# Attention inside a hybrid decoder layer: values as matmul weights in two column halves, four blocks at a time, then turned back

## The chip, the cores and the metric

The kernel runs on one core of a Trainium2 chip. The core has a matmul engine (TensorE, "PE" in the profile; its weight loads are listed apart as "PEld"), a vector engine (DVE), a scalar engine (ACT), GpSimd (POOL) and a queue engine (SP) that here only issues DMAs. Each engine runs its own instructions in order and they meet at semaphores. The metric is the device time of one whole execution in microseconds; lower is better.

## The reference

One layer at sequence length 2048 and width 1024, all in fp32: RMSNorm, one projection, eight retention heads beside eight heads of dilated sliding-window attention, output projection, then a SwiGLU block. The change touches only the attention:

```python
# per pattern (window, dilation) in (128,1), (512,4), (2048,16); blocks of 128 queries
s = einsum('brhnqd,brhnkd->brhnqk', qb, kcat) * (D ** -0.5)   # own block of keys and the one before
s = where(mask, s, -inf); m = max(s); p = exp(s - m); den = sum(p)
o = einsum('brhnqk,brhnkd->brhnqd', p, vcat) / den
lse = m + log(den)
# then: w = softmax(stack(lses)); out = sum(w * stack(outs))
```

## The kernel before

Three stages follow each other on the core: the projection (`project`, to about 555 us), the attention (`attention`, to about 849 us), and the rest (`mix`: retention, combination, output projection; `ffn`).

`attention` works on pairs of heads. There are NU = 4 pairs ("units") and, for each, NB = 48 blocks of 128 queries: 16 of dilation 1, 16 of dilation 4, 16 of dilation 16; so ALL = 192 blocks, numbered n. A block with a block of keys before it has two key blocks of 128 ("full": 27 of the 48, namely 15 of the first 16 and 12 of the next 16), the others have one ("half": 21, and all of the last 16). Per block n:

- `scores(n)` on PE (L763): for two heads, two matmuls each with the queries as weights and the keys as the moving operand (fp32r), into one of NS = 3 PSUM banks.
- DVE (L822): scales, adds the mask, takes the minimum of the negated scores, writes `prob[n % 4]` and the minimum into `orow[n % RING]`; waits for `turned` of block n-4 because `prob` has four buffers.
- ACT (L851): exp over `prob`, two instructions.
- `turn(n)` on PE (L775): 2 or 4 transposes of `prob` into one of TURNED = 3 banks. It waits for exp of block n and for the copy of block n-3.
- `copy_turned(n)`: PSUM to `probT`; even blocks on DVE (L813), odd blocks on ACT (L841). On DVE it stands right behind the maxima of block n+2, so DVE waits there for the turn.
- `values(n)` on PE (L787): `probT` as weights (128 columns), the values with a column of ones beside each head as moving operand (65 columns, fp32): 2 or 4 matmuls, each shown as two passes. The ones give the denominator.
- `copy_out(n)` on ACT (L845): result and denominator (130 columns) into `orow`; SP stores the row block to `att_out` (L714).

The order on PE is written out by hand: in step n, `scores(n+4)`, `turn(n+1)`, `values(n-1)`. On DVE: maxima of n, then (n even) `copy_turned(n-2)`; in the last unit also `early_vector`, which for even j from 24 to 40 (not 32) rounds an eighth of the next stage's weights (L1127). On ACT: exp of n, then (n odd) `copy_turned(n-2)`, then `copy_out(n-4)`. POOL reorders queries and keys for the dilated patterns beside all this (L881 to L885).

`mix` uses the matmul array in tiles in two places: L1253 with `tile_position=(h*32, 0)` (32 rows by 128 columns, 128 moving columns) and L1229 with `tile_position=(0, h*32)` (128 rows by 32 columns, 64 moving columns), both fp32.

Of the kernel before, what the change touches and what calls it, by code (L numbers as in the profile page):

```python
# [9 lines left out]
ACT = mybir.ActivationFunctionType  # L10
# [4 lines left out]
P = 128  # L15
# [7 lines left out]
ATT_HEADS, ATT_D = 8, 64  # L23
# [623 lines left out]
def attention(nc, D, bank, first, mixed):  # L647
# [6 lines left out]
    NU = ATT_HEADS // 2  # L654
    ALL = NU * NB
    SCALE = ATT_D ** -0.5
    NS, AHEAD, TURNED = 3, 4, 3
    RING = 16
    OW = ATT_D + 1
    NEAR = CHUNKS  # L660
    m = Mem(nc, None, "at")
    ident, mask, vblk = (first[n] for n in ("ident", "mask", "vblk"))
# [1 line left out]
    def place(name, shape, frame, offset=0, dt=F32):  # L664
        return nc.alloc_sbuf_tensor_at(f"at_{name}", shape, dt, offset=FRAMES + frame * FRAME + offset)
# [2 lines left out]
    k_by4 = place("k_by4", [P, 2, 2, SEQ], 8, dt=F32R)  # L668
    q_by16 = place("q_by16", [P, 2, SEQ], 12, dt=F32R)
    prob = place("prob", [P, 4, 2, 2 * P], 14)  # L670
    probT = place("probT", [P, TURNED, 2, 2, P], 15)
    orow = place("orow", [P, RING, AO_W], 15, 6144)
    s_ps = bank[:, 0:NS, :].rearrange("p n (h k) -> p n h k", h=2)
    t_ps = bank[:, NS:NS + TURNED, :].rearrange("p n (h b q) -> p n h b q", h=2, b=2)
    o_ps = bank[:, NS + TURNED:8, :].rearrange("p n (h k) -> p n h k", h=2)
    consts, qk_first, qk_rest, v_loaded = (first[n] for n in ("consts", "qk_first", "qk_rest", "v_loaded"))
    permuted = m.sem("permuted")
    scored, maxed, exped = m.sem("scored"), m.sem("maxed"), m.sem("exped")
    turned = m.sem("turned")
    turn_copied = m.sems("turn_copied", 2)  # L680
    valued, o_copied = m.sem("valued"), m.sem("o_copied")
    waited = m.sem("waited")
    stored = m.sems("stored", RING)

    C_O = 2
    C_SCORED, C_PERMUTED = 1, 1
    BY_4, BY_16 = 6, 8
    keys = [slice(0, 2 * P) if b[3] else slice(P, 2 * P) for b in blocks]
# [20 lines left out]
    def sync(sp):  # L709
        def store(u, j):  # L710
            p, t0, d, _ = blocks[j]
            sp.wait_ge(o_copied, NB * u + j + 1 + C_O)
            dst = D["att_out"][p, t0:t0 + d * (P - 1) + 1:d, :]
            sp.dma_start(dst[:, bass.ds(u * AO_W, AO_W)], orow[:, j % RING, :]).then_inc(stored[j % RING], 16)  # L714

        def unit(u, s, more=True):

            sp.wait_ge(permuted, BY_16 * u + C_PERMUTED)
            sp.sem_inc(waited, 1)
            sp.wait_ge(scored, NB * u + C_SCORED)  # L720
            sp.sem_inc(waited, 1)
            for j in range(NB):
                store(u, j)
                if more:
                    for n in range(2 * QK_DMAS):
                        if (n // 2 if n < QK_DMAS else QK_DMAS // 2 + 5 * (n - QK_DMAS) // 2) == j:
                            load_qk(sp, D, first, u + 1, 1 - s, n)
                if more and j and j % 4 == 0:
                    load_values(sp, D, first, u + 1, j // 4 - 1)
                if not more:  # L730
                    mixed["early_sync"](sp, j, permuted, BY_16 * NU + C_PERMUTED)
            if more:
                load_values(sp, D, first, u + 1, VALUE_LOADS - 1)

        for r, free in enumerate(first["row_free"]):
            sp.wait_ge(free, first["rows_stored"])
        with sp.Fori(0, NU // 2 - 1) as it:
            unit(2 * it, 0)
            unit(2 * it + 1, 1)
        unit(NU - 2, 0)  # L740
        unit(NU - 1, 1, more=False)

    def copied(eng, n):
        eng.wait_ge(turn_copied[n % 2], n // 2 + 1)

    def tensor(pe):
        pe.sem_inc(scored, C_SCORED)

        def scores(n):
            u, j = divmod(n, NB)  # L750
            if j == 0:
                pe.wait_ge(qk_first, 16 * QK_DMAS * u + 16 * QK_DMAS)
            if j == GROUP // P:
                pe.wait_ge(qk_rest, 16 * QK_DMAS * u + 16 * QK_DMAS)
            if j == NEAR:
                pe.wait_ge(permuted, BY_16 * u + BY_4 + C_PERMUTED)
            if j == 2 * NEAR:
                pe.wait_ge(permuted, BY_16 * u + BY_16 + C_PERMUTED)
            if n >= NS:
                pe.wait_ge(maxed, n - NS + 1)  # L760
            for h in range(2):
                for lower in range(2):
                    last = nc.tensor.matmul(s_ps[:, n % NS, h, keys[j]], query(u % 2, j, h), key(u % 2, j, h, lower),  # L763
                                            start=lower == 0, stop=lower == 1)
            last.then_inc(scored, 1)

        def turn(n):
            j = n % NB
            pe.wait_ge(exped, n + 1)
            if n >= TURNED:  # L770
                copied(pe, n - TURNED)
            for h in range(2):
                for kb in range(2):
                    if kb == 1 or blocks[j][3]:
                        last = nc.tensor.transpose(t_ps[:, n % TURNED, h, kb, :], prob[:, n % 4, h, kb * P:(kb + 1) * P], ident[:])  # L775
            last.then_inc(turned, 1)

        def values(n):
            u, j = divmod(n, NB)
            if j % 4 == 0:  # L780
                pe.wait_ge(v_loaded[j // 4], 16 * u + 16)
            copied(pe, n)
            pe.wait_ge(o_copied, n + 1)
            first = 0 if blocks[j][3] else 1
            for h in range(2):
                for kb in range(first, 2):
                    last = nc.tensor.matmul(o_ps[:, n % 2, h, 0:OW], probT[:, n % TURNED, h, kb, :], vblk[:, j - 1 + kb, h, :],  # L787
                                            start=kb == first, stop=kb == 1)
            last.then_inc(valued, 1)

        for n in range(AHEAD):
            scores(n)
        turn(0)
        for n in range(ALL):
            if n + AHEAD < ALL:
                scores(n + AHEAD)
            if n + 1 < ALL:
                turn(n + 1)
            if n:
                values(n - 1)  # L800
        values(ALL - 1)

    def vector(dve):
        for r in range(RING):
            dve.sem_inc(stored[r], 16)
        dve.wait_ge(consts, 16)

        def copy_turned(n):
            if n >= TURNED:
                dve.wait_ge(valued, n - TURNED + 1)  # L810
            dve.wait_ge(turned, n + 1)
            kb = 0 if blocks[n % NB][3] else 1
            nc.vector.tensor_copy(probT[:, n % TURNED, :, kb:, :], t_ps[:, n % TURNED, :, kb:, :]).then_inc(turn_copied[0], 1)  # L813

        for n in range(ALL):
            j = n % NB
            dve.wait_ge(scored, n + 1 + C_SCORED)
            if n >= 4:
                dve.wait_ge(turned, n - 3)
            dve.wait_ge(stored[n % RING], 16 * (n // RING) + 16)  # L820
            for h in range(2):
                last = nc.vector.tensor_tensor_reduce(  # L822
                    out=prob[:, n % 4, h, keys[j]], in0=s_ps[:, n % NS, h, keys[j]], in1=mask[:, keys[j]],
                    scale=-SCALE, scalar=-3 * NEG, op0=ALU.add, op1=ALU.min,
                    accum_out=orow[:, n % RING, 2 * OW + h:2 * OW + h + 1])
            last.then_inc(maxed, 1)
            if n >= 2 and n % 2 == 0:
                copy_turned(n - 2)
            if n >= ALL - NB:
                mixed["early_vector"](dve, j, permuted, BY_16 * NU + C_PERMUTED)  # L830
        copy_turned(ALL - 2)

    def scalar(act):
        act.sem_inc(o_copied, C_O)

        def copy_turned(n):
            if n >= TURNED:
                act.wait_ge(valued, n - TURNED + 1)
            act.wait_ge(turned, n + 1)
            kb = 0 if blocks[n % NB][3] else 1  # L840
            nc.scalar.activation(probT[:, n % TURNED, :, kb:, :], t_ps[:, n % TURNED, :, kb:, :], ACT.Copy).then_inc(turn_copied[1], 1)  # L841

        def copy_out(n):
            act.wait_ge(valued, n + 1)
            nc.scalar.activation(orow[:, n % RING, 0:2 * OW].rearrange("p (h c) -> p h c", h=2), o_ps[:, n % 2, :, 0:OW], ACT.Copy).then_inc(o_copied, 1)  # L845

        for n in range(ALL):
            act.wait_ge(maxed, n + 1)
            for h in range(2):
                pr = prob[:, n % 4, h, keys[n % NB]]  # L850
                last = nc.scalar.activation(pr, pr, ACT.Exp, bias=orow[:, n % RING, 2 * OW + h:2 * OW + h + 1], scale=-1.0)  # L851
            last.then_inc(exped, 1)
            if n >= 2 and n % 2 == 1:
                copy_turned(n - 2)
            if n >= 4:
                copy_out(n - 4)
        copy_turned(ALL - 1)
        for n in range(ALL - 4, ALL):
            copy_out(n)

    def gpsimd(pool):
        pool.sem_inc(permuted, C_PERMUTED)
# [1664 lines left out]
```

## Time and profile before

| | us |
|---|---|
| median of 3 runs | 2446.33 (2446.18 to 2450.53) |
| the profiled execution | 2445.58 |
| its span (first to last instruction) | 2443.8 |
| attention, about | 556 to 849 |

Busy time over the span is 2380.5 us (97%) on PE, 1429.3 (58%) on DVE, 926.1 (38%) on ACT and 596.0 (24%) on POOL. A matmul instruction of fp32 operands appears as two passes, each with a weight load. The duration of a pass includes its way through the array, and passes overlap, so the cost of one is the distance between the starts of two, not its duration. In a timeline, equal neighbours are merged into one row: its start, the time from the first start to the last end, and the count; the last one starts one duration before the row's end.

### The profile page before, as it was taken

How to read it: one execution, taken by the hardware profiler on the slowest of the kernel's cores; microseconds unless marked ns; L12 is line 12 of the kernel's file. 1: busy time of each engine (PE TensorE's matmuls, PEld its weight loads, DVE VectorE, ACT ScalarE, POOL GpSimd, SP SyncE). 2: the span in 40 equal slices, each digit the busy share in tenths (PEclk: the TensorE clock that was granted, in tenths of full speed). 3: DMA queues.
4: the chain of work that ended last, by engine and by line, in shares of the span. 5: the costliest groups of instructions: out<-in, count | busy, mean ns of one | idle time of the engine just before them, and what ended most of it. 6: DMA issues, size and time to landing. Idle time of an engine off the chain costs nothing. (4 is left out here: it accounts for less than half of the span.)

```text
span 2443.8 us, 35931 instructions
## 1 busy us (share of the span) xinstructions
PE 2380.5 (97%) x12432; PEld 2019.1 (83%) x12432; DVE 1429.3 (58%) x2671; ACT 926.1 (38%) x1790; POOL 596.0 (24%) x365
## 2 busy tenths in 40 slices
PE   7999999999999989999899999989999999999998
PEld 6888888889999978887788888878888887888887
DVE  4322346635555568788666656776665665455655
ACT  4401122217777613234433333533333343322332
POOL 0089555525553456662000000000000000000001
PEclk9999999999999979999999999999999999999999
DMA  5423224466776445555333333433333335445655
GB/s 182 128 77 108 69 75 114 120 185 175 182 177 176 136 151 178 191 181 203 125 95 105 103 106 107 129 124 91 106 93 117 107 112 202 142 146 197 235 205 188
DMA packets 308890, 344.92 MB, mean 141 GB/s; under 512 B 17072, under 2 KB 239920, under 8 KB 308528
## 3 DMA queue, kind: packets, MB, share of 16 engines
q1 hardware_dynamic: 308784, 343.54, 45.9%
q8 instruction: 62, 1.02, 0.2%
q14 instruction: 44, 0.36, 0.1%
HBM read 231.41 MB, written 112.07 MB: 141 GB/s over the span
## 5 line engine op out<-in xcount | busy, mean ns | idle before, releaser
L1812 PE MATMUL fin_psum_bank<-ff_b_hi,ff_w_hi 128*128 128x512 f32 x1232 | 482.4, 392 | 18.7 <-issue 8.6
L1812 PE MATMUL fin_psum_bank<-ff_b_hi,ff_w_lo 128*128 128x512 f32 x1232 | 481.4, 391 | 0.0
L1812 PE MATMUL fin_psum_bank<-ff_b_lo,ff_w_hi 128*128 128x512 f32 x1232 | 481.3, 391 | 0.0
L2111 POOL TENSOR_TENSOR ff_ssq<-ff_ssq,ff_minus_half 128x1 f32<-128x1 f32 x16 | 14.8, 926 | 1265.8 <-DVE ff_ssq L2379 1265.8
L1812 PEld LDWEIGHTS fin_psum_bank<-ff_b_hi,ff_w_hi 128*128 128x128 f32 x1232 | 232.7, 189 | 69.3 <-issue 9.0
L1812 PEld LDWEIGHTS fin_psum_bank<-ff_b_lo,ff_w_hi 128*128 128x128 f32 x1232 | 232.7, 189 | 48.5
L1812 PEld LDWEIGHTS fin_psum_bank<-ff_b_hi,ff_w_lo 128*128 128x128 f32 x1232 | 232.4, 189 | 48.7
L1894 PE MATMUL fin_psum_bank<-ff_down_hi,ff_act_hi 128*128 128x512 f32 x616 | 240.4, 390 | 2.2 <-DVE ff_act_lo L2143 2.2
L1894 PE MATMUL fin_psum_bank<-ff_down_hi,ff_act_lo 128*128 128x512 f32 x616 | 240.3, 390 | 0.0
L1894 PE MATMUL fin_psum_bank<-ff_down_lo,ff_act_hi 128*128 128x512 f32 x616 | 240.2, 390 | 0.0
L2115 DVE TENSOR_TENSOR ff_w_lo<-ff_raw,ff_w_hi 128x512 fp32r<-128x512 f32 x176 | 120.9, 688 | 145.6 <-ACT ff_w_hi L1905 145.5
L460 PE MATMUL pr_psum_acc<-pr_hT_hi,pr_w_hi 128*128 128x512 f32 x512 | 199.2, 389 | 0.0
L460 PE MATMUL pr_psum_acc<-pr_hT_lo,pr_w_hi 128*128 128x512 f32 x512 | 199.2, 389 | 0.0
L460 PE MATMUL pr_psum_acc<-pr_hT_hi,pr_w_lo 128*128 128x512 f32 x512 | 199.2, 389 | 0.0
L851 ACT ACTIVATE at_prob<-at_prob,at_orow 128x256 f32<-128x256 f32 (+1 forms) x384 | 155.4, 454 | 36.3 <-DVE at_orow L822 35.1
L1953 ACT ACTIVATE ff_taken<-fin_psum_bank 128x512 f32<-128x512 f32 x132 | 78.9, 597 | 227.1 <-PE fin_psum_bank L1812 222.1
L1925 ACT ACTIVATE ff_act_hi<-ff_act_raw 128x1408 fp32r<-128x1408 f32 x56 | 77.4, 1382 | 216.3 <-DMA ff_act_raw<-a_parts 216.3
L787 PE MATMUL fin_psum_bank<-vblk,at_probT 128*128 128x65 f32 x1200 | 155.4, 267 | 0.3
L1905 ACT ACTIVATE ff_w_hi<-ff_raw 128x512 fp32r<-128x512 f32 x176 | 109.9, 627 | 108.0 <-PE fin_psum_bank L1812 103.0
L787 PEld LDWEIGHTS fin_psum_bank<-vblk,at_probT 128*128 128x128 f32 x1200 | 148.9, 192 | 1.1 <-ACT at_probT L841 0.9
L2115 DVE TENSOR_TENSOR ff_w_lo<-ff_sums,ff_w_hi 128x512 fp32r<-128x512 f32 x132 | 90.6, 689 | 91.5 <-ACT ff_w_hi L1905 91.5
L822 DVE CUSTOM_DVE_ANT_0 at_prob<-fin_psum_bank,mask 128x256 f32<-128x256 f32 (+1 forms) x384 | 119.8, 360 | 36.0 <-PE fin_psum_bank L763 34.5
(206 smaller groups left out, 4557.8 us busy)
## 6 DMA issues: line engine op xcount, KB each, us to landing
ff_act_raw<-a_parts SPq DMA_DIRECT2D x56, 704.0 KB, 4.1
ff_raw<-in_w_gate SPq DMA_DIRECT2D x22, 1024.0 KB, 5.9
ff_raw<-in_w_up SPq DMA_DIRECT2D x22, 1024.0 KB, 5.3
a_parts<-ff_a_sum SPq DMA_DIRECT2D x88, 256.0 KB, 6.1
ff_down_raw<-in_w_down SPq DMA_DIRECT2D x77, 256.0 KB, 4.7
a_parts<-ff_up SPq DMA_DIRECT2D x66, 256.0 KB, 2.3
att_out<-at_orow SPq DMA_DIRECT2D x192, 66.0 KB, 3.0
mx_att_in<-att_out SPq DMA_DIRECT2D x16, 792.0 KB, 4.8
```

Source lines behind the costliest of these rows:

```text
L460: last = nc.tensor.matmul(acc[:, g, :], w[s][:, k, :], h[:, k, t], start=k == 0 and n == 0, stop=k == KT - 1 and n == 2)
L787: last = nc.tensor.matmul(o_ps[:, n % 2, h, 0:OW], probT[:, n % TURNED, h, kb, :], vblk[:, j - 1 + kb, h, :], start=kb == first, stop=kb == 1)
L822: last = nc.vector.tensor_tensor_reduce(out=prob[:, n % 4, h, keys[j]], in0=s_ps[:, n % NS, h, keys[j]], in1=mask[:, keys[j]], scale=-SCAL ...
L851: last = nc.scalar.activation(pr, pr, ACT.Exp, bias=orow[:, n % RING, 2 * OW + h:2 * OW + h + 1], scale=-1.0)
L1812: last = nc.tensor.matmul(to, w[:, i, k, :], b[i][:, k, :], start=fresh and k == 0 and which == 0, stop=k == KH - 1 and which == 2, skip_g ...
L1894: last = nc.tensor.matmul(bank[:, ORDER[n], :], a[t % 3][:, k, :], w[o % 2][k][:], start=k == 0 and which == 0, stop=k == PAIRS - 1 and wh ...
L1905: nc.scalar.activation(w_hi[:, i], weight(i, s), ACT.Copy).then_inc(w_hi_done[i], 1)
L1925: nc.scalar.activation(act_hi[t % 3][:], act_raw[t % 3][:], ACT.Copy).then_inc(act_hi_done, 1)
L1953: nc.scalar.activation(taken[:, i, :], X[s], ACT.Copy).then_inc(snapped, 1)
L2111: nc.gpsimd.tensor_tensor(ssq[:, n % 2, 1:2], ssq[:, n % 2, 1:2], minus_half[:], ALU.pow).then_inc(rooted, 1)
L2115: nc.vector.tensor_tensor(w_lo[:, i], weight(i, s), w_hi[:, i].bitcast(F32), ALU.subtract).then_inc(w_lo_done[i], 1)
```

## The change

`values` now works on quads of four blocks. The values become the weights, 64 columns for each head, head 0 in columns 0 to 63 of the array and head 1 in columns 64 to 127 (`tile_position=(0, h * ATT_D)`), and `probT` is the moving operand (128 columns). The result of a quad is one PSUM bank `oT_ps`, with the head's dimensions on the partitions. DVE copies it to SBUF (`lift`), PE turns it back with four transposes (`turn_back`), and ACT copies four row blocks at once into `orow` (`copy_out`). The denominator is no longer a column of ones: the exp instruction sums its output itself (`accum_out`). `probT` gets KEPT = 6 buffers instead of 3.

```diff
-        def values(n):
-            ...
-            copied(pe, n)
-            pe.wait_ge(o_copied, n + 1)
-            for h in range(2):
-                for kb in range(first, 2):
-                    last = nc.tensor.matmul(o_ps[:, n % 2, h, 0:OW], probT[:, n % TURNED, h, kb, :], vblk[:, j - 1 + kb, h, :],
-                                            start=kb == first, stop=kb == 1)
+        def values(q):
+            if q:
+                pe.wait_ge(lifted, q)
+            ...
+            for i in range(QUAD):
+                n, j = QUAD * q + i, j0 + i
+                copied(pe, n)
+                first = 0 if blocks[j][3] else 1
                 for kb in range(first, 2):
+                    for h in range(2):
+                        rows = slice(h * ATT_D, (h + 1) * ATT_D)
+                        last = nc.tensor.matmul(oT_ps[rows, i * P:(i + 1) * P], vblk[:, j - 1 + kb, h, 1 - h:1 - h + ATT_D],
+                                                probT[:, n % KEPT, h, kb, :], start=kb == first, stop=kb == 1,
+                                                tile_position=(0, h * ATT_D), skip_group_check=True)
+        def turn_back(q):
+            pe.wait_ge(lifted, q + 1)
+            if q:
+                pe.wait_ge(o_copied, q)
+            for i in range(QUAD):
+                last = nc.tensor.transpose(o_ps[:, i, :], oT[:, q % 2, i * P:(i + 1) * P], ident[:])
...
-            if n:
-                values(n - 1)
+            if n % QUAD == 0 and n:
+                values(n // QUAD - 1)
+            if n % QUAD == 2 and n > QUAD + 2 - 1:
+                turn_back(n // QUAD - 1)
...
+        def lift(q):
+            if q >= 2:
+                dve.wait_ge(turned_back, q - 1)
+            dve.wait_ge(valued, q + 1)
+            nc.vector.tensor_copy(oT[:, q % 2, :], oT_ps[:]).then_inc(lifted, 1)
+
+        LIFT = 9
         for n in range(ALL):
             j = n % NB
+            if n >= LIFT and n % QUAD == LIFT % QUAD:
+                lift((n - LIFT) // QUAD)
             dve.wait_ge(scored, n + 1 + C_SCORED)
...
+        def copy_out(q):
+            act.wait_ge(turned_back, q + 1)
+            at = QUAD * q % RING
+            nc.scalar.activation(orow[:, at:at + QUAD, 1:1 + 2 * ATT_D], o_ps[:], ACT.Copy).then_inc(o_copied, 1)
+
+        OUT = 10
         for n in range(ALL):
             act.wait_ge(maxed, n + 1)
             for h in range(2):
-                last = nc.scalar.activation(pr, pr, ACT.Exp, bias=orow[:, n % RING, 2 * OW + h:2 * OW + h + 1], scale=-1.0)
+                last = nc.scalar.activation(pr, pr, ACT.Exp, bias=orow[:, n % RING, LEAST + h:LEAST + h + 1], scale=-1.0,
+                                            accum_out=orow[:, n % RING, SUMS[h]:SUMS[h] + 1])
             last.then_inc(exped, 1)
             if n >= 2 and n % 2 == 1:
                 copy_turned(n - 2)
-            if n >= 4:
-                copy_out(n - 4)
+            if n >= OUT and n % QUAD == OUT % QUAD:
+                copy_out((n - OUT) // QUAD)
```

The stores on SP wait for the quad's copy instead of the block's. After the loops DVE runs `copy_turned(190)`, `lift(46)`, `lift(47)`; PE runs `values(47)`, `turn_back(47)`; ACT runs `copy_turned(191)`, `copy_out(46)`, `copy_out(47)`.

## Rows read from the trace of the kernel before

**Rows 1.** The page: busy time of each engine, its share of the span, instructions.

```profile
PE 2380.5 (97%) x12432; PEld 2019.1 (83%) x12432; DVE 1429.3 (58%) x2671; ACT 926.1 (38%) x1790; POOL 596.0 (24%) x365
```

**Rows 2.** A unit by stretch: length, busy of PE, PEld, DVE, ACT, POOL; clock.

```profile
604.00:676.00 72.00, 72.00 (x643) 72.00 (x641) 41.24 (x217) 56.91 (x168) 30.88 (x8) 1.00 0.76 178
```

**Rows 3.** Groups by line and form, 556 to 849: count, busy us, mean ns.

```profile
L787 PE MATMUL fin_psum_bank<-vblk,at_probT 128*128 128x65 f32 x1200 | 155.4, 267 | 0.3
L775 PE MATMUL fin_psum_bank<-at_ident,at_prob 128*128 128x128 f32 x600 | 98.9, 275 | 0.2
...
L813 DVE COPY at_probT<-fin_psum_bank 128x512 f32<-128x512 f32 x44 | 30.4, 692 | 66.2 <-PE fin_psum_bank L775 66.2
L813 DVE COPY at_probT<-fin_psum_bank 128x256 f32<-128x256 f32 x52 | 22.1, 424 | 46.2 <-PE fin_psum_bank L775 46.2
...
L1127 DVE CAST mx_w_hi<-mx_w_out 128x1024 fp32r<-128x1024 f32 x8 | 8.5, 1064 | 0.0
```

**Rows 4.** Timeline of PE, 668 to 672: start, length, line, shapes, count.

```profile
668.95 0.72 PE L763 MATMUL fin_psum_bank<-at_k_by,at_q_by 128*128 128x256 f32 x4
669.50 0.60 PE L775 MATMUL fin_psum_bank<-at_ident,at_prob 128*128 128x128 f32 x4
669.95 1.00 PE L787 MATMUL fin_psum_bank<-vblk,at_probT 128*128 128x65 f32 x8
670.76 0.72 PE L763 MATMUL fin_psum_bank<-at_k_by,at_q_by 128*128 128x256 f32 x4
```

**Rows 5.** Timelines of PE and PEld around the column tiles of L1229.

```profile
1008.37 0.83 PE L1219 MATMUL fin_psum_bank<-mx_qkv,mx_probT 128*128 128x64 f32 x6
1009.14 0.43 PE L1229 MATMUL fin_psum_bank<-mx_qkv,mx_k_dec 128*32 128x64 f32 x16
...
1009.13 0.27 PEld L1229 LDWEIGHTS fin_psum_bank<-mx_qkv,mx_k_dec 128*32 128x32 f32 x16
```

**Rows 6.** Timeline of PE around the row tiles of L1253.

```profile
999.01 0.38 PE L1245 MATMUL fin_psum_bank<-at_ident,mx_qkv 128*128 128x128 f32 x2
999.32 0.73 PE L1253 MATMUL fin_psum_bank<-mx_qkv 32*128 32x128 f32 x16
999.98 0.50 PE L1294 MATMUL fin_psum_bank<-mx_w_hi,mx_mT_hi 128*128 128x512 f32 x1
```

**Rows 7.** Those lines alone: durations in ns, minimum, median, maximum.

```profile
L1229 PE MATMUL fin_psum_bank<-mx_qkv,mx_k_dec x256: 219/219/317, 857.0 to 1113.1; 128*32 128x64 f32 x128
...
L1253 PE MATMUL fin_psum_bank<-mx_qkv x256: 270/270/577, 850.2 to 1103.5; 32*128 32x128 f32 x128
```

**Rows 8.** Timelines of PE and DVE around one copy of a turned block.

```profile
661.62 0.60 PE L775 MATMUL fin_psum_bank<-at_ident,at_prob 128*128 128x128 f32 x4
...
662.34 0.69 DVE L813 COPY at_probT<-fin_psum_bank 128x512 f32<-128x512 f32 x1 [1.83 <-PE fin_psum_bank L775]
662.94 0.41 DVE L822 CUSTOM_DVE_ANT_0 at_prob<-fin_psum_bank,mask 128x256 f32<-128x256 f32 x1
```

**Rows 9.** Waits of DVE, 556 to 849: total us, times, longest.

```profile
DVE at_probT L813 <- PE fin_psum_bank L775: 112.4, 93, 1.8
```

**Rows 10.** Timeline, 845 to 847: PE restarting behind ACT.

```profile
845.62 0.69 ACT L851 ACTIVATE at_prob<-at_prob,at_orow 128x128 f32<-128x128 f32 x2 [0.27 <-DVE at_orow L822]
...
846.37 0.44 PE L775 MATMUL fin_psum_bank<-at_ident,at_prob 128*128 128x128 f32 x2
```

**Rows 11.** Timeline of ACT: an instruction that sums its output.

```profile
1149.60 0.19 ACT L1066 ACTIVATION_READ_ACCUMULATOR mx_rows<-fin_psum_bank 128x1 f32 x1
1149.69 1.91 ACT L1933 ACTIVATE ff_b_hi<-ff_b_sum 128x2048 fp32r<-128x2048 f32 x1
```

**Rows 12.** Timeline of ACT, 702 to 704: exps of a full block.

```profile
702.52 0.91 ACT L851 ACTIVATE at_prob<-at_prob,at_orow 128x256 f32<-128x256 f32 x2 [0.54 <-DVE at_orow L822]
703.34 0.36 ACT L841 ACTIVATE at_probT<-fin_psum_bank 128x256 f32<-128x256 f32 x1
```

**Rows 13.** The stretch behind the attention; the clock stands third from the end.

```profile
851.70:882.40 30.70, 21.99 (x127) 18.17 (x128) 16.73 (x34) 2.79 (x7) 16.70 (x14) 0.50 0.55 178
```

More of the change, by code:

```diff
@@ L656, in attention @@
     SCALE = ATT_D ** -0.5
-    NS, AHEAD, TURNED = 3, 4, 3
+    NS, AHEAD, TURNED, KEPT = 3, 4, 3, 6
+    QUAD = 4
+    QUADS = ALL // QUAD
     RING = 16
-    OW = ATT_D + 1
+    SUMS, LEAST = (0, 2 * ATT_D + 1), 2 * ATT_D + 2
     NEAR = CHUNKS
@@ L670, in attention @@
     prob = place("prob", [P, 4, 2, 2 * P], 14)
-    probT = place("probT", [P, TURNED, 2, 2, P], 15)
+    probT = place("probT", [P, KEPT, 2, 2, P], 22)
+    oT = place("oT", [P, 2, QUAD * P], 15)
     orow = place("orow", [P, RING, AO_W], 15, 6144)
@@ L674, in attention @@
     t_ps = bank[:, NS:NS + TURNED, :].rearrange("p n (h b q) -> p n h b q", h=2, b=2)
-    o_ps = bank[:, NS + TURNED:8, :].rearrange("p n (h k) -> p n h k", h=2)
+    oT_ps = bank[:, NS + TURNED, :]
+    o_ps = bank[:, 7, :].rearrange("p (n c) -> p n c", n=QUAD)
     consts, qk_first, qk_rest, v_loaded = (first[n] for n in ("consts", "qk_first", "qk_rest", "v_loaded"))
@@ L680, in attention @@
     turn_copied = m.sems("turn_copied", 2)
-    valued, o_copied = m.sem("valued"), m.sem("o_copied")
+    valued, lifted, turned_back, o_copied = m.sem("valued"), m.sem("lifted"), m.sem("turned_back"), m.sem("o_copied")
     waited = m.sem("waited")
     stored = m.sems("stored", RING)
-    C_O = 2
     C_SCORED, C_PERMUTED = 1, 1
@@ L711, in store @@
             p, t0, d, _ = blocks[j]
-            sp.wait_ge(o_copied, NB * u + j + 1 + C_O)
+            sp.wait_ge(o_copied, NB // QUAD * u + j // QUAD + 1)
             dst = D["att_out"][p, t0:t0 + d * (P - 1) + 1:d, :]
@@ L776, in turn @@
             last.then_inc(turned, 1)
-        def values(n):
-            u, j = divmod(n, NB)
-            if j % 4 == 0:
-                pe.wait_ge(v_loaded[j // 4], 16 * u + 16)
-            copied(pe, n)
-            pe.wait_ge(o_copied, n + 1)
-            first = 0 if blocks[j][3] else 1
-            for h in range(2):
-                for kb in range(first, 2):
-                    last = nc.tensor.matmul(o_ps[:, n % 2, h, 0:OW], probT[:, n % TURNED, h, kb, :], vblk[:, j - 1 + kb, h, :],
-                                            start=kb == first, stop=kb == 1)
-            last.then_inc(valued, 1)
+        def values(q):
+            if q:
+                pe.wait_ge(lifted, q)
+            u, j0 = divmod(QUAD * q, NB)
+            pe.wait_ge(v_loaded[j0 // 4], 16 * u + 16)
+            for i in range(QUAD):
+                n, j = QUAD * q + i, j0 + i
+                copied(pe, n)
+                first = 0 if blocks[j][3] else 1
+                for kb in range(first, 2):
+                    for h in range(2):
[3 more added lines that the diff above has]
+                                                tile_position=(0, h * ATT_D), skip_group_check=True)
+            last.then_inc(valued, 1)
+        def turn_back(q):
[4 more added lines that the diff above has]
+                last = nc.tensor.transpose(o_ps[:, i, :], oT[:, q % 2, i * P:(i + 1) * P], ident[:])
+            last.then_inc(turned_back, 1)
         for n in range(AHEAD):
@@ L798, in tensor @@
                 turn(n + 1)
-            if n:
-                values(n - 1)
-        values(ALL - 1)
+            if n % QUAD == 0 and n:
+                values(n // QUAD - 1)
+            if n % QUAD == 2 and n > QUAD + 2 - 1:
+                turn_back(n // QUAD - 1)
+        values(QUADS - 1)
+        turn_back(QUADS - 1)
     def vector(dve):
@@ L808, in copy_turned @@
         def copy_turned(n):
-            if n >= TURNED:
-                dve.wait_ge(valued, n - TURNED + 1)
+            if n >= KEPT:
+                dve.wait_ge(valued, (n - KEPT) // QUAD + 1)
             dve.wait_ge(turned, n + 1)
             kb = 0 if blocks[n % NB][3] else 1
-            nc.vector.tensor_copy(probT[:, n % TURNED, :, kb:, :], t_ps[:, n % TURNED, :, kb:, :]).then_inc(turn_copied[0], 1)
+            nc.vector.tensor_copy(probT[:, n % KEPT, :, kb:, :], t_ps[:, n % TURNED, :, kb:, :]).then_inc(turn_copied[0], 1)
+        def lift(q):
[4 more added lines that the diff above has]
+        LIFT = 9
         for n in range(ALL):
             j = n % NB
+            if n >= LIFT and n % QUAD == LIFT % QUAD:
+                lift((n - LIFT) // QUAD)
             dve.wait_ge(scored, n + 1 + C_SCORED)
@@ L824, in vector @@
                     scale=-SCALE, scalar=-3 * NEG, op0=ALU.add, op1=ALU.min,
-                    accum_out=orow[:, n % RING, 2 * OW + h:2 * OW + h + 1])
+                    accum_out=orow[:, n % RING, LEAST + h:LEAST + h + 1])
             last.then_inc(maxed, 1)
@@ L831, in vector @@
         copy_turned(ALL - 2)
+        lift(QUADS - 2)
+        lift(QUADS - 1)
     def scalar(act):
-        act.sem_inc(o_copied, C_O)
         def copy_turned(n):
-            if n >= TURNED:
-                act.wait_ge(valued, n - TURNED + 1)
+            if n >= KEPT:
+                act.wait_ge(valued, (n - KEPT) // QUAD + 1)
             act.wait_ge(turned, n + 1)
             kb = 0 if blocks[n % NB][3] else 1
[L841 to L845, printed above, removed]
+            nc.scalar.activation(probT[:, n % KEPT, :, kb:, :], t_ps[:, n % TURNED, :, kb:, :], ACT.Copy).then_inc(turn_copied[1], 1)
+        def copy_out(q):
[3 more added lines that the diff above has]
+        OUT = 10
         for n in range(ALL):
@@ L854, in scalar @@
                 copy_turned(n - 2)
-            if n >= 4:
-                copy_out(n - 4)
+            if n >= OUT and n % QUAD == OUT % QUAD:
+                copy_out((n - OUT) // QUAD)
         copy_turned(ALL - 1)
-        for n in range(ALL - 4, ALL):
-            copy_out(n)
+        copy_out(QUADS - 2)
+        copy_out(QUADS - 1)
     def gpsimd(pool):
```

## Prediction

> **What bounds the kernel now.** The page first: PE is busy for 97% of the span, no other engine for more than 58% [rows 1]. That is an average over stages, so the attention is read by units of 48 blocks: each takes 72.0 us, PE busy 72.00 of them, DVE 41, ACT 57, at clock 1.00 [rows 2]. The three whole units between 604 and 820 look alike. The waits agree: DVE waited 112.4 us in the attention for turns, 93 times for 96 copies [rows 9]. So PE sets the pace, and DVE stands ready behind each turn of an even block. That second fact matters as much as the first.
>
> **Prices on PE.** Distances between starts: four transposes are one row of 0.60 us with 0.275 for the last, so (0.60 - 0.275)/3 = 0.109 each; four scores take 0.55 (668.95 to 669.50), 0.137 each, right behind a value pass. Behind a transpose, where the new order puts most of them, their load is better hidden; between 0.109 and 0.137 I take 0.118 [rows 3, 4]. Eight value passes go from 669.95 to 670.76: 0.81 us although only 65 columns move, of which the first costs least; a further one is 0.112, four are 0.37 [rows 4]. The unit adds up: 192 scores at 0.137 (26.4), 150 transposes at 0.109 (16.4), 27 x 0.81 + 21 x 0.37 for the values (29.6) are 72.4; the trace has 72.0.
>
> **Values, new form.** No row shows tiles of 64 columns. The nearest are those of L1229, four tiles of 32 columns, 64 columns moving. Sixteen passes start within 0.43 - 0.219 = 0.21 us [rows 5, 7], where the full array needs 0.112 for every one. So they go four at a time, in four rounds: three distances of some 0.06 and the stagger. For 128 moving columns L1253 has sixteen passes starting within 0.73 - 0.27 = 0.46 us: its first round is longer by some 0.1 (nothing hides its load), so a round is 0.11 [rows 6]. I take pairs (two heads) at 0.110 a round: 150 rounds a unit, 16.5 us for 29.6, a gain of 13.1. Ends: pairs don't overlap (300 x 0.110 = 33.0, 3 lost), or a round is as cheap as L1229's 0.06 (9 us, gain 21); the price goes with the columns moved, so I stay near 0.110.
>
> A rule of the Trainium skill speaks against this. "TensorE: Matmul & The Clock Gate", Part 3, says a weight load overlaps matmuls in flight only if its row group differs, and both halves here use all rows. The trace disagrees: the sixteen loads of L1229, all on the same rows, lie within 0.27 us beside sixteen passes [rows 5]. It is rival D.
>
> **Changing the array's form.** Before L1229 the last full pass starts at 1008.37 + 0.83 - 0.275 = 1008.93, the first tile at 1009.14: 0.21 for 0.112 [rows 5]. Before L1253 it is 999.12 to 999.32, 0.20, and its load is then exposed; behind it the last tile starts at 999.32 + 0.73 - 0.27 = 999.78, the next full load at 999.98, and that pass lasts 0.50 instead of 0.39, another 0.10 [rows 6]. With a load of 64 columns (0.05, half of the 0.10 for 128) entry costs 0.15 more than an ordinary neighbour, exit 0.19: 0.34 a quad, 12 quads, 4.1 us a unit. Bounds: 0.1 (drains that overlap) to 0.45.
>
> **Turning back** is 48 transposes a unit, 48 x 0.109 = 5.2 us. The new unit on PE without waits is 22.7 (scores at 0.118) + 16.4 + 16.5 + 4.1 + 5.2 = 64.9, a gain of 7.1 us on 72.0; scores at 0.109 or 0.137 make it 63.2 or 68.6.
>
> **The new wait.** In step 4q+6 PE does `scores(4q+10)`, `turn(4q+7)`, then `turn_back(q)`, which needs `lift(q)`. On DVE `lift(q)` stands ahead of the maxima of block 4q+9, right behind `copy_turned(4q+6)`, and that copy needs `turn(4q+6)`, which PE did just one step before. From the start X of the last transpose of that turn (661.62 + 0.60 - 0.27 = 661.95): the copy starts at X + 0.38 (662.34); what follows it on DVE 0.60 later (662.94) [rows 8]; the lift has the same form as that copy and takes 0.69 [rows 3]; PE resumes 0.06 behind a releaser (846.31 to 846.37) [rows 10], with a first load that nothing hides, 0.06. Sum: X + 1.79. PE is ready at X + 0.11 + 4 x 0.118 + 4 x 0.109 = X + 1.02. So **PE stands still for 0.77 us in each quad**. Where the blocks are half: copy distance 0.34 (0.424 less the same overlap of 0.08), turn 0.22: X + 1.52 against X + 0.80, 0.72. A unit has 8 and 4 of them: 8 x 0.77 + 4 x 0.72 = 9.0 us. Queued behind the waiting `turn_back` are the next scores and turn, so nothing on PE fills it. The wait is larger than the gain. If it were covered, what is late next is ACT.
>
> **ACT** in a full quad: two exps take 0.82 a block (702.52 to 703.34) [rows 12], each sum read adds 0.09 (1149.60 to 1149.69) [rows 11], so 1.00; two copies of a turned block 1.0, one copy-out 0.5: 5.5 us a quad for PE's 4 x 1.46 + 0.34 + 0.77 = 6.95. It is off the path as a whole. Tight is one place: behind the lift come the maxima of 4q+9 (0.77), its exps (1.10), then PE's `turn(4q+9)`: about X + 3.6, and PE arrives at X + 1.79 + 0.44 + 0.47 + 0.44 + 0.47 = X + 3.61. A tie; I take nothing, at most 0.4 a full quad. It is rival E. The lifts (0.6 us a quad) fit DVE's idle share.
>
> **The rest.** In the last unit `early_vector` puts a rounding between the copy and the lift at j = 24, 28, 36 and 40: 4 x 1.06 less 0.08 is 3.9 us more wait [rows 3]; those roundings were hidden behind DVE's waits before. Tail: values, lift, turn back and copy follow each other with nothing beside them: 0.15 + 0.89 + 0.3 + 0.69 + 0.1 + 0.7 + 0.5 against the last copies of before; about 2 us more, 0 to 4. Stores go in fours, six blocks ahead of the reuse of their `orow` buffer instead of twelve: six blocks are 7 to 10 us, so nothing. `probT`'s six buffers free before they are asked for. Behind the attention the clock was 0.50 (1.2 GHz) for 30.7 us, after a stretch of low use [rows 13]; it may begin or end elsewhere: plus or minus 4.
>
> **Sum** against the profiled execution's 2445.58 (0.75 below the median): 4 x (9.0 - 7.1) = 7.6, + 3.9, + 2: 2459.1; as a median 2460.
>
> **The rivals.**
> A, the forecast: 2452 to 2468 by the bounds of the form change and tail.
> B, the other side: the wait is covered. It decides at one point: copy and lift done within PE's 1.02 us, 0.77 sooner than the rows give. Then PE's gain is left: 2445.6 - 4 x 7.1 + 2 + 0.75, **2420**. For it only that nothing in the trace shows a lift; against it the 93 waits.
> C, no pairs: the halves run one behind the other, 4 x 16.5 = 66 more: **2526**. Against it [rows 5].
> D, loads exposed: 600 rounds x 0.05: **2490**.
> E, ACT's chain behind the lift is late as well, by 0.4 in 32 full quads, or sum reads cost their whole 0.19: **2474**.
> F, changing form costs 0.1 instead of 0.34, 48 x 0.24 = 11.5 less: **2448**, no difference.
>
> **How the numbers follow.** A 0.48, B 0.14, C 0.05, D 0.06, E 0.13, F 0.14. The likeliest is 2460. A range from 2440 to 2490 leaves out B and C, 0.19. Faster or slower means by over 0.2% (4.9 us), about what can be told from no change: faster 0.14 (B), same 0.14 (F), slower 0.72 (A, C, D, E).
>
> **What would show it.** `turn_back` should be preceded by PE idle of 0.6 to 0.8 us, 48 times, released by DVE's lift; the value passes should start in pairs, rounds 0.11 apart; 0.2 us between forms; PE busy per unit down from 72 to about 65 and the unit near 74. Wrong if that idle is missing, if lifts start before the turn of block 4q+6, or if the rounds are 0.16 or more apart.

## The result, and the profile after

| | before | after |
|---|---|---|
| median, us | 2446.59 (2446.18 to 2450.53) | 2479.82 (2478.21 to 2480.91) |
| the profiled execution | 2445.58 | 2478.93 |
| its span | 2443.8 | 2477.1 |
| attention, first matmul to last | 555.7 to 848.4 | 555.3 to 880.3 |

The changed kernel takes 1.0132 times as long [1.0114, 1.0149], 33 us more, where the sum of the forecast has 13.5 (7.6 + 3.9 + 2). All of it lies between the start of the attention and the start of the next stage's matmuls, 294.1 us before and 328.0 after; the rest is 0.6 shorter. The page shows little of that: PE is busy for 2373.5 us of a longer span [against rows 1].

```profile
PE 2373.5 (96%) x12624; PEld 1981.1 (80%) x12624; DVE 1452.1 (59%) x2719; ACT 938.4 (38%) x2030; POOL 596.3 (24%) x365
```

The units of 48 blocks show it. Each row is one of the four units of the changed kernel (the last to the next stage's start): its stretch and length, busy of PE, PEld, DVE, ACT and POOL, then the granted clock.

```profile
555.30:634.20 78.90, 68.95 (x643) 61.56 (x644) 45.47 (x220) 56.79 (x214) 30.73 (x8) 0.94 0.58 145
634.20:712.90 78.70, 70.18 (x693) 62.06 (x692) 47.74 (x228) 60.01 (x230) 30.99 (x8) 0.98 0.66 165
712.90:791.60 78.70, 70.24 (x694) 62.12 (x692) 47.75 (x228) 59.72 (x230) 30.89 (x8) 0.98 0.67 163
791.60:883.40 91.80, 76.39 (x739) 66.31 (x737) 55.84 (x244) 64.10 (x244) 51.11 (x19) 0.95 0.45 134
```

The kernel before has 72.1 us at clock 1.00 for the second unit and 78.4 for the last:

```profile
627.10:699.20 72.10, 72.10 (x644) 72.10 (x643) 41.34 (x217) 56.82 (x169) 30.80 (x9) 1.00 0.73 178
...
771.40:849.80 78.40, 76.83 (x670) 75.37 (x670) 49.72 (x230) 58.83 (x179) 50.89 (x19) 1.00 0.49 142
```

PE is now idle for 8.5 us in a middle unit, against 0.0, and its clock mean is 0.98. Units grew by 7.5, 6.5, 6.5 and 13.4 us; the forecast had 1.9, 1.9, 1.9 and 7.8. So **some 5 us a unit are not in the sum**.

The waits of the changed kernel, 550 to 900 us, name two causes (who waited, for whom: total us, times, longest):

```profile
POOL at_k_by L911 <- DMA k_near<-rot_lo: 186.9, 4, 49.2
...
PEld fin_psum_bank L803 <- DVE at_oT L837: 39.7, 48, 1.7
...
PE fin_psum_bank L803 <- DVE at_oT L837: 28.3, 48, 1.5
...
PE fin_psum_bank L766 <- POOL at_q_by L913: 9.3, 4, 3.9
```

L803 is `turn_back`, L837 is `lift`: the forecast wait, 48 times. The last row is new. L766 is `scores` (L763 before): at block 16 of every unit PE waits for the queries and keys that POOL reorders. Timeline of PE there, second unit (start, length, line, shapes, count, idle before and releaser):

```profile
658.91 0.60 PE L778 MATMUL fin_psum_bank<-at_ident,at_prob 128*128 128x128 f32 x4
661.59 0.67 PE L766 MATMUL fin_psum_bank<-at_k_by,at_q_by 128*128 128x128 f32 x4 [2.08 <-POOL at_q_by L913]
```

And right behind each such wait the clock is at 1.2 GHz. Stretches of the changed kernel in units 3 and 4, clock third from the end:

```profile
741.60:744.90 3.30, 3.30 (x31) 2.97 (x28) 0.00 (x0) 1.32 (x6) 3.30 (x2) 0.50 0.75 146
...
820.10:823.40 3.30, 3.30 (x29) 2.97 (x26) 0.00 (x0) 1.09 (x5) 3.30 (x2) 0.50 0.40 105
```

Unit 2 has the same at 663.1 (3.4 us), unit 1 has 6.8 us at 581.1. PE works all through them, at half speed.

Why is POOL late? Its own timelines, before and then after. Before, the reordering starts 0.25 us ahead of the unit (it was ready earlier, and waits for PE's `scores`); after, 3.61 us into it (634.24), released by a DMA:

```profile
626.81 15.73 POOL L881 CAST at_k_by<-k_near 128x2048 fp32r<-128x2048 f32 x4 [39.32 <-PE fin_psum_bank L763]
642.45 7.87 POOL L883 CAST at_q_by<-q_near 128x2048 fp32r<-128x2048 f32 x2
```

```profile
637.85 15.84 POOL L911 CAST at_k_by<-k_near 128x2048 fp32r<-128x2048 f32 x4 [49.16 <-DMA k_near<-rot_lo]
653.55 7.98 POOL L913 CAST at_q_by<-q_near 128x2048 fp32r<-128x2048 f32 x2
```

The six copies end at 661.53 and PE's scores start at 661.59. Before, they ended at 650.32 and PE came at 652.35: a margin of 2.0 us. The DMA that POOL waits for is the last load of the keys. Its issue on SP, before and after:

```profile
618.16 0.47 SPq L102 DMA_DIRECT2D k_near<-rot_lo  x1
```

```profile
632.28 0.47 SPq L102 DMA_DIRECT2D k_near<-rot_lo  x1
```

It was issued 8.9 us ahead of the unit's start and is now 2.0 us ahead of it. In SP's list that load stands behind the store of block 33, `5 * (n - QK_DMAS) // 2` in the code, and a store now waits for its quad's `copy_out`, some steps later than the copy of one block.

### The profile page after: what moved, and what is told of

Its sections match the earlier page's. It is cut to its first block and busy times, and to the rows that moved or that the text cites. A ratio compares the mean times of both kernels' runs of the same rounds, so it can differ in the third digit from the quotient of the medians.

```text
span 2477.1 us, 36548 instructions
## 1 busy us (share of the span) xinstructions
PE 2373.5 (96%) x12624; PEld 1981.1 (80%) x12624; DVE 1452.1 (59%) x2719; ACT 938.4 (38%) x2030; POOL 596.3 (24%) x365
## 5 line engine op out<-in xcount | busy, mean ns | idle before, releaser
L880 ACT ACTIVATE at_prob<-at_prob,at_orow 128x256 f32<-128x256 f32 (+1 forms) x384 | 172.9, 454 | 79.5 <-DVE at_orow L849 79.2
L1924 PEld LDWEIGHTS fin_psum_bank<-ff_down_hi,ff_act_hi 128*128 128x128 f32 x616 | 115.6, 188 | 26.4 <-DVE ff_act_lo L2173 2.5
L1924 PEld LDWEIGHTS fin_psum_bank<-ff_down_hi,ff_act_lo 128*128 128x128 f32 x616 | 115.6, 188 | 24.2
```

What stands on the lines that cost most here:

```text
L1924: last = nc.tensor.matmul(bank[:, ORDER[n], :], a[t % 3][:, k, :], w[o % 2][k][:], start=k == 0 and which == 0, stop=k == PAIRS - 1 and wh ...
```

## The experiments

Two theories stood at the start. L: the excess over the forecast is the loads that stand behind gated stores. Rival: the form of the passes or the lift's wait cost more than the forecast took. Each kernel below is the changed one with the edit shown, unless the text says otherwise. A second rival is in the expectation of the first run: that the clock falls by itself, whatever PE waits for. The medians of the kernel before, run beside them on the same chip, were 2447.57 and, for the last two, 2449.09. The changed kernel's 2479.82 was measured beside one of 2446.59 and not again, so a difference from it can be off by some 1 us (2.5 for the last two).

**Loads earlier.** The last loads of queries and keys stand behind earlier stores; nothing else is touched.

```diff
-    if (n // 2 if n < QK_DMAS else QK_DMAS // 2 + 5 * (n - QK_DMAS) // 2) == j:
+    if (n // 2 if n < QK_DMAS else QK_DMAS // 2 + 3 * (n - QK_DMAS) // 2) == j:
```

> The changed kernel, but the loads of the next unit's queries and keys stand earlier in SP's list (the last behind the store of block 22 instead of 33). Theory L (the loads sit behind stores that now wait for a quad, so GpSimd starts its reordering 3.6 us into the unit, PE waits for it at block 16 and its clock then falls): in units 2 to 4 GpSimd starts within 0.5 us of the unit, has its first six copies done 23.9 us into it, PE comes at 25.0 and does not wait; about 4.1 us a unit come back, 12 us, 2467 to 2469; the first unit keeps its wait. Rival K (the clock falls because of the attention's own lower use, not because of that wait): the falls to 1.2 GHz near block 16 stay, only the waits of 2 us go, 2473 to 2475. Rival N (the loads are not the cause): 2480.

Measured: 2469.0 us (2468.27 to 2470.09), 1.0084 [1.0067, 1.0101]. One third of the loss is gone with one number in SP's list. The second unit's POOL, PE at its block 16, and the two middle units:

```profile
635.52 15.81 POOL L911 CAST at_k_by<-k_near 128x2048 fp32r<-128x2048 f32 x4 [46.19 <-PE fin_psum_bank L766]
```

```profile
660.00 0.60 PE L778 MATMUL fin_psum_bank<-at_ident,at_prob 128*128 128x128 f32 x4
660.36 0.64 PE L766 MATMUL fin_psum_bank<-at_k_by,at_q_by 128*128 128x128 f32 x4
```

```profile
635.30:710.10 74.80, 68.33 (x694) 60.61 (x692) 48.09 (x228) 59.98 (x230) 31.11 (x8) 1.00 0.70 171
710.10:785.20 75.10, 68.28 (x693) 60.56 (x691) 47.82 (x228) 59.80 (x229) 31.10 (x8) 1.00 0.69 170
```

POOL is again released by PE, the wait at block 16 is gone (0.36 between the two starts), the clock is 1.00, and the units take 74.8 and 75.1 us where the forecast had 64.9 + 9.0 = 73.9. Theory L holds for these units, and rival K (the clock falls by itself) falls with them. The first unit keeps its wait (3.9 us) and 6.8 us of low clock behind it, since its keys are loaded before the attention.

**Late stores alone, in the kernel before.** The reverse: nothing on PE, DVE or ACT is edited, and each store waits for about the copy that it waits for in the changed kernel.

```diff
-            sp.wait_ge(o_copied, NB * u + j + 1 + C_O)
+            sp.wait_ge(o_copied, NB * u + j // 4 * 4 + 7 + C_O if more or j < 44 else NB * u + 48 + C_O)
```

> The kernel before, but each store waits until the block that ends its quad's step in the changed kernel is copied (three to six blocks later), and with it the loads behind it in SP's list. Nothing on PE, DVE or ACT is edited. Theory L: GpSimd starts 3 to 4 us into units 2 to 4, PE waits some 2 us at block 16 in each and its clock falls: 2453 to 2460. Rival N (lateness of the loads costs nothing): 2446 to 2448.

Measured: 2463.98 us (2458.58 to 2471.27), 1.0056 [1.0036, 1.0077]: 16 us, more than the expectation's upper end. Its waits, one unit, and a stretch behind the wait at block 16 of the second unit:

```profile
PE fin_psum_bank L763 <- POOL at_q_by L883: 8.8, 4, 2.7
```

```profile
631.00:708.80 77.80, 75.56 (x645) 75.42 (x644) 41.63 (x217) 57.43 (x171) 30.75 (x8) 0.96 0.70 167
...
659.10:665.80 6.70, 6.70 (x34) 6.70 (x34) 1.89 (x9) 1.80 (x6) 6.70 (x2) 0.50 0.84 200
```

The same row PE <- POOL appears in a kernel whose compute engines run the old code, with about the same total (8.8 for 9.3), and the clock falls behind it. So SP's order alone is enough to bring on the wait and the falls; no new pass is needed. But the loads are not all of the 16 us. The profiled execution is the longest of the four (2471.27), and its units are 4.3, 5.6, 3.1 and 9.5 us longer than before. The first of these is not SP's: its loads come before the attention (below). Of the last, 2.85 us stand at its very end and come from the stores themselves, of which more are still to be issued when the last copy is done. Issue of the last stores on SP, before and in this run:

```profile
846.78 2.60 SPq L714 DMA_DIRECT2D att_out<-at_orow  x5
```

```profile
865.52 5.99 SPq L714 DMA_DIRECT2D att_out<-at_orow  x10
```

They end at 849.38 and 871.51, and PE's first matmul of the next stage starts 0.45 us behind both (849.83 and 871.96), which is 1.42 and 4.27 us behind its last value pass. DVE also waits 2.7 us for row buffers that late stores still read; the kernel before has no such wait. Moving the loads (the run above) leaves these two alone; what each is of the 16 us was not tried.

**Lift earlier.** DVE does `lift(q)` behind the maxima of block 4q+8, ahead of `copy_turned(4q+6)`, so that it no longer stands behind the copy that needs PE's last turn.

```diff
-        LIFT = 9
+        LIFT = 8
         for n in range(ALL):
-            if n >= LIFT and n % QUAD == LIFT % QUAD:
-                lift((n - LIFT) // QUAD)
...
+            if n >= LIFT and n % QUAD == LIFT % QUAD:
+                lift((n - LIFT) // QUAD)
             if n >= 2 and n % 2 == 0:
                 copy_turned(n - 2)
```

> The changed kernel, but DVE copies the quad's result one step earlier: behind the maxima of block 4q+8 and ahead of the copy of turned block 4q+6. Theory: PE no longer stands before each turn back (48 times 0.65 to 0.70 us, and 3 us more where a rounding stood between), 35 to 40 us of waits go; but PE then comes to block 16 some 3 us sooner while GpSimd is ready no sooner, so 3 us a unit are waited there instead: net 22 to 30 us, 2450 to 2458. If DVE's order is not what makes PE wait: 2480. If the waits only move to the scores or the exps: 2465 to 2480.

Measured: 2464.22 us (2463.35 to 2466.44), 1.0063 [1.0047, 1.008]. The gain is 15.6 us, less than expected, and next to the case in which the waits only move (2465 to 2480). The waits tell why:

```profile
PE fin_psum_bank L766 <- POOL at_q_by L913: 21.3, 4, 5.8
...
PE fin_psum_bank L803 <- DVE at_oT L837: 1.8, 3, 0.9
```

The lift's wait is gone, 28.3 to 1.8 us. PE comes to block 16 that much sooner, and waits there longer for a POOL that is no faster: 9.3 became 21.3, and the clock falls for 6.8 us in all four units instead of one. PE's waits for exps (L778) rose as well, from 0.6 to 5.8 us. Two waits in a row of the same unit: taking one away feeds the other.

**Both edits.**

> Both edits on the changed kernel: lift one step earlier and loads earlier. Theory: all 48 waits before the turns back go and the loads land in time; what is left is GpSimd's own 23.6 us for six copies against PE at about 22 us: a wait of 1 to 2 us a unit, with a fall of the clock where it is longest: 2436 to 2446, so no slower than the kernel before. If the form changes and turns back eat the gain of the pairs: 2446 or more.

Measured: 2447.79 us (2445.46 to 2449.37), 1.0001 [0.9992, 1.0011]: no difference from the kernel before, and 1.8 us above the expected range. The third row of waits below is ACT's exp, the fourth DVE waiting for a row buffer (`orow`) that a store still reads; then the second unit:

```profile
PE fin_psum_bank L766 <- POOL at_q_by L913: 9.8, 4, 5.8
...
PE fin_psum_bank L803 <- DVE at_oT L837: 1.1, 2, 0.9
...
PEld fin_psum_bank L778 <- ACT at_prob L880: 11.4, 29, 0.7
...
DVE at_prob L847 <- DMA att_out<-at_orow: 13.4, 17, 1.6
```

```profile
629.10:698.40 69.30, 66.77 (x691) 60.83 (x690) 48.86 (x228) 60.01 (x229) 31.24 (x8) 1.00 0.75 185
```

The pair of edits takes back 32 of the 33 us: with both waits treated, a middle unit takes 69.4 us, 2.8 less than before. So the gain of the pairs is not eaten, though the number alone would fit that case too (2446 or more). The last unit takes 81.1 against 78.4: the tail is still there (1.7 us), the last turn back waits 0.9 for its lift, and PE waits 2.5 us for exps against 1.2 in a middle unit, among the roundings; these were not tried apart. The first unit keeps 6.1 us between the two starts at block 16. POOL is the bound up to block 16 even now: 24.0 us from the unit's start to its scores, 23.6 of them the six copies.

**The heads apart.** Only the order of the value passes: both key blocks of head 0, then both of head 1.

```diff
-                for kb in range(first, 2):
-                    for h in range(2):
+                for h in range(2):
+                    for kb in range(first, 2):
```

> The changed kernel, but within a block all products of head 0 come before those of head 1, so neighbours no longer alternate between the two column halves. If the engine takes passes strictly in order and overlaps only neighbours of different halves: a full block needs 6 rounds of 0.11 us instead of 4, 108 blocks x 0.22 = 23.5 us more: 2500 to 2506. If it runs the halves in parallel whatever the order: 2479 to 2482. If the halves never overlapped, no change either, but then the passes would not start 7 ns apart as they do.

Measured: 2480.28 us, a single execution. The same quad of 14 matmuls (28 passes) in the changed kernel and here:

```profile
684.80 1.75 PE L793 MATMUL fin_psum_bank<-at_probT,vblk 128*64 128x128 f32 x28
```

```profile
689.73 1.80 PE L793 MATMUL fin_psum_bank<-at_probT,vblk 128*64 128x128 f32 x28
```

A full block costs no more here than its four rounds: passes in strict order with only neighbours overlapping would have cost 5.9 us a unit (27 blocks x 0.22). The starts are now 0.052 and 0.057 apart for the most part instead of 0.007 and 0.102. The total alone says less than it seems to, since in the attention of this profile the clock is at 1.2 GHz for 10 us less than in that of the changed kernel. But its second unit, at clock 1.00, takes 77.3 us with 2.2 between the starts at block 16, and that of the run with early loads 74.8 with none: 0.4 us apart. So between these two orders the price hardly differs. No row names the half that a pass is in, so this run by itself doesn't exclude passes that go one by one at 0.055 each; for halves that work at the same time speak the starts 7 ns apart in the changed kernel.

**Queries first.** On top of both edits, POOL begins with the two query copies. Their buffer `q_by4` is last read 16 blocks ahead of the unit's end, so they can start 7 us before the next unit does. The four key copies come behind them, after the wait for the last scores of the previous unit.

```diff
-    C_SCORED, C_PERMUTED = 1, 1
+    C_SCORED, C_PERMUTED = 17, 1
...
+                pool.wait_ge(scored, NB * u - 16 + C_SCORED)
+                pool.sem_inc(waited, 1)
+                for h in range(2):
+                    nc.gpsimd.tensor_copy(by(q_by4, h, 4), near(q_near[h], 4)).then_inc(permuted, 1)
...
-                for h in range(2):
-                    nc.gpsimd.tensor_copy(by(q_by4, h, 4), near(q_near[h], 4)).then_inc(permuted, 1)
```

> On top of both edits, GpSimd reorders the queries for dilation 4 first and as soon as the previous unit's dilation-4 scores are done, so that in units 2 to 4 only the four key copies (16 us) are left at the unit's start. Theory (what is left of the wait at block 16 in those units is GpSimd's own 24 us against PE's 22): PE's waits of 1.6 us before block 16 go in units 2 to 4, unit periods fall from 69.4 to 67 to 68 us, the first unit keeps its wait of some 6 us; 2438 to 2444, 0.2 to 0.4% under the kernel before. Rival (PE then waits for exps or for row buffers instead): the same time as with both edits, 2446 to 2449.

Measured: 2446.04 us (2442.78 to 2449.49) against 2449.09, 0.9986 [0.9976, 0.9996]: the only version faster than the kernel before, by 0.14%. POOL in the second unit (its start 630.9), that unit, and what DVE then waits for:

```profile
623.63 8.02 POOL L910 CAST at_q_by<-q_near 128x2048 fp32r<-128x2048 f32 x2 [33.62 <-DMA k_near<-rot_lo]
631.59 15.92 POOL L915 CAST at_k_by<-k_near 128x2048 fp32r<-128x2048 f32 x4
```

```profile
630.90:701.80 70.90, 68.12 (x694) 61.07 (x692) 49.04 (x228) 60.59 (x229) 31.32 (x9) 1.00 0.75 182
```

```profile
DVE at_prob L847 <- DMA att_out<-at_orow: 20.2, 25, 1.7
```

The copies are ready 16.6 us into the unit instead of 24, and PE comes to block 16 after 22.5 instead of 24.0. Yet the unit takes 70.9 for 69.4: the time comes back as waits for row buffers (20.2 us instead of 13.4) and for exps (13.4 instead of 11.4). The rival of this run, that the waits only move, is right for the middle units. The profile's four units together are no shorter than with both edits alone (295.7 and 294.4), so where the 0.14% comes from stays open, and that this version beats the one with both edits isn't shown: their intervals overlap.

## Why the prediction was right and wrong

**The bound, and the pairs: right.** The halves work at the same time. In the row of 684.80 fourteen pairs start within 1.75 - 0.27 = 1.48 us, thirteen distances of 0.114; pair by pair most are 0.109, the two starts of one 7 ns apart. Forecast 0.110. Rival C falls. Rival D falls too: the loads of all 1200 passes (137 ns each at the median) fit between starts 0.109 apart. The Trainium skill's rule in "TensorE: Matmul & The Clock Gate", Part 3, that a load overlaps matmuls in flight only where the row group differs, isn't borne out here either; all loads are on the same rows.

**Changing form: the size was too high.** Before the quad, 684.22 + 0.66 - 0.27 = 684.61 to 684.80 is 0.19; behind it, 686.28 to 686.48 is 0.20. Against 0.109 for a neighbour that is some 0.17 a quad. The first pair of a quad also stands 0.160 from the second, so from transposes to scores it is about 0.24 for the 0.34 forecast. Timeline of PE from there on, the changed kernel:

```profile
684.22 0.66 PE L778 MATMUL fin_psum_bank<-at_ident,at_prob 128*128 128x128 f32 x4
...
686.48 0.74 PE L766 MATMUL fin_psum_bank<-at_k_by,at_q_by 128*128 128x256 f32 x4
687.06 0.60 PE L778 MATMUL fin_psum_bank<-at_ident,at_prob 128*128 128x128 f32 x4
687.41 0.72 PE L766 MATMUL fin_psum_bank<-at_k_by,at_q_by 128*128 128x256 f32 x4
687.97 0.60 PE L778 MATMUL fin_psum_bank<-at_ident,at_prob 128*128 128x128 f32 x4
689.11 0.66 PE L803 MATMUL fin_psum_bank<-at_ident,at_oT 128*128 128x128 f32 x4 [0.53 <-DVE at_oT L837]
```

Four scores and four transposes take 0.93 (686.48 to 687.41); forecast 0.91.

**The lift's wait: right, in place, cause and count.** The last transpose starts at 687.97 + 0.60 - 0.27 = 688.30 and `turn_back` at 689.11: 0.81, so 0.70 of standing still in a full quad and 0.65 in a half one, for 0.77 and 0.72. DVE shows the chain as worked out, copy, lift, maxima:

```profile
687.76 0.69 DVE L831 COPY at_probT<-fin_psum_bank 128x512 f32<-128x512 f32 x1 [2.37 <-PE fin_psum_bank L778]
688.37 0.68 DVE L837 COPY at_oT<-fin_psum_bank 128x512 f32<-128x512 f32 x1
688.97 0.41 DVE L849 CUSTOM_DVE_ANT_0 at_prob<-fin_psum_bank,mask 128x256 f32<-128x256 f32 x1
```

This unit sums to 8 x 0.70 + 4 x 0.65 = 8.2 us of wait. In the run with early loads 74.8 - 8.2 = 66.6 is left as PE's work, for 64.9 forecast and within its 63.2 to 68.6. The starts on PE in that unit (635.33 to 710.09) split the 1.7. Only 23 of the 48 groups of four scores stand right behind a turn; the other 24 behind value passes and turns back take 0.56 on average, where all were priced at 0.47: 2.0 more. Waits for exps add 1.0 (next paragraph). The form change takes 1.1 off, turns back and rounds 0.4. That makes 1.5 of the 1.7. Rival B falls: the lift came 0.70 us too late, and with the lift moved the wait was gone, which shows its cause.

**ACT's tie, roundings, tail.** Rival E is seen in small: PE's loads waited for exps 5.1 us in 22 places in the attention of the changed kernel. In five quads of each unit the turn ahead of the value passes starts 0.15 late and takes 0.06 longer, so 0.2 in five places a unit, where E had 0.4 in eight and the forecast nothing. The roundings lengthened the distance to `turn_back` in their four quads to 1.42, 1.41, 1.36 and 1.76, together 2.7 us more than 0.81 for 3.9 forecast. The gap to the next stage is 3.14 us for 1.42, a tail of 1.7 for the 2 forecast. The size is partly luck: the forecast's chain ends with ACT's copy, which is done at 881.17, while the next stage starts 0.44 behind SP's issue of the last store (882.95), a term that it didn't have.

**The step that failed** is the sentence "Stores go in fours, six blocks ahead of the reuse of their `orow` buffer instead of twelve: ... so nothing." It asked only who waits for the stored buffer. It did not ask what is queued behind the waiting store on SP, and there `load_qk` and `load_values` of the next unit stand. In "POOL reorders ... beside all this" the second half of the error lies: POOL needs 23.6 us for what PE asks for 25 us into a unit, so its margin of 2.0 us (650.32 to 652.35 in the kernel before) was less than the delay of the load (POOL starts 3.6 us into the unit instead of 0.25 before it). In the run with both edits a faster PE used the margin up by itself. The late loads are 3.9 us in unit 2 and 3.5 in unit 3 (78.7 in the changed kernel, 74.8 and 75.1 with early loads) and 3.4 in the last (91.8 to 88.4): 10.8 of the 20 us that the sum lacks.

**What is left of the 20.** The profiled execution with early loads (2469.64) stands 10.5 us above the sum's 2459.1: 6.3 in the first unit, 2.2 in the last, 1.7 in the middle ones, 0.3 outside. In the first unit POOL started 2.85 us in (0.91 in the profile of before), and so it did in the profiles of the changed kernel and of all experiments, that of the late stores in the old kernel too (2.6 to 3.6); the loads it needs are issued before any code that was changed. So of the 4.15 us between starts there (0.755 before), 1.9 are the landing, and the rest is that PE now comes to block 16 sooner. The clock was at 1.2 GHz for 3.4 us right behind the unit's start (558.1) and for 6.8 behind that wait: from block 16 on, this unit takes 53.2 us and a middle one of the same run 49.7, so 3.5 us are the clock. In the last unit the roundings make four distances of 1.4 to 1.8 us, and behind the longest the clock is at 1.2 GHz for 3.4 us (858.5; in the changed kernel 867.9), at most 1.7 us lost. Why the landing varies was not tried.

**The clock** was forecast only as plus or minus 4 behind the attention. It was 0.50 for 34.1 us there, from 881.5, which is 1.9 us ahead of the next stage; before, it was 30.7 us from 851.7, 1.9 us behind the stage's start. Since all outside the attention is 0.6 us shorter, no loss is seen:

```profile
881.50:915.60 34.10, 22.69 (x142) 18.57 (x143) 16.85 (x32) 2.75 (x6) 16.68 (x14) 0.50 0.51 165
```

The falls inside the attention were in no case of the forecast. One that follows a wait nearly doubles it: 2 us of standing still, then 3.4 us at half speed, which is 1.7 more where PE has work all through.

The direction was right, for the forecast's own reason in part. That the range held the time was luck: its upper end, 2490, is the time of rival D, which falls, and 2479.8 lies 12 us above the 2452 to 2468 of the forecast's own mechanism. Of the 33 us, some 18 are the steps of its sum, where it had 13.5 (1.7 of the difference is the clock in the last unit), 11 are the loads behind the stores, and some 5 are the first unit's wait for POOL and the clock behind it, neither of which it had looked at.

## What to carry to other kernels

When a change makes an instruction wait longer or later, list all that stands behind it in its own queue, a DMA queue above all: here stores that wait longer made the old kernel 16 us slower with nothing else changed, in part through the loads behind them, in part because the next stage starts behind the last store. Before an engine is made faster, read the margin of every engine that feeds it (start of use less end of production), since the gain stops where the smallest of these is used up. A wait that is taken away is worth only what the next one leaves: 26 us of waits for DVE gone brought 15.6 us, and the loads moved as well another 16.4.

## What the runs showed of the hardware

Two column halves of the array with 64 columns each, fp32, 128 columns moving, cost 0.109 us for a pair of passes. One pass of the full array costs 0.109 with 128 columns moving (the transposes) and 0.112 with 65. The price was the same with the halves alternating and with one behind the other within a block. Going to this form and back costs 0.19 and 0.20 us from start to start.

PE's clock fell to 1.2 GHz for 3.4 or 6.8 us, at most 1.9 us behind the wait, after most single waits of 2 to 3 us within otherwise dense work, but not after all. At block 16 there were nine of 1.9 to 2.9 us in these profiles: it fell behind seven (units 2 to 4 of the changed kernel, 1, 2 and 4 of the late stores in the old kernel, 3 of the heads apart) and not behind two, the 2.2 and 2.8 us in units 2 and 4 of the heads apart. Of four waits of 1.6 us it fell behind one (late stores, unit 3) and not behind three (both edits). What decides was not tried. (These are distances between starts; the idle time that a row shows is 0.3 less.) Unit 4 of the heads apart, the wait and then the clock:

```profile
819.11 0.66 PE L766 MATMUL fin_psum_bank<-at_k_by,at_q_by 128*128 128x128 f32 x4 [2.57 <-POOL at_q_by L913]
```

```profile
819.20:826.00 6.80, 6.26 (x68) 5.68 (x68) 3.12 (x14) 2.42 (x10) 6.80 (x2) 1.00 0.84 273
```

An exp that also sums its output shows a second ACT instruction of 0.19 us, of which 0.09 to 0.10 count in the distance to the next. Timeline of ACT, the changed kernel:

```profile
687.76 0.19 ACT L880 ACTIVATION_READ_ACCUMULATOR at_prob<-at_prob,at_orow 128x1 f32 x1
687.86 0.40 ACT L880 ACTIVATE at_prob<-at_prob,at_orow 128x128 f32<-128x128 f32 x1
```
